# Moving the operands of the matrix products by 32 to 96 bytes in SBUF

## What is computed

```
for l in range(DEPTH):                       # DEPTH = 2
    h = hybrid_mixer(x, w_in[l], ...)        # three branches, three gates, one output projection
    x = layer_norm(alpha * x + h, ...)
    h = memory_cross_attention(x, mem, ...)  # 4 heads of 256
    x = layer_norm(alpha * x + h, ...)
    h = conv_ffn(x, ffn_w_in[l], ...)        # 1024 -> 2 x 2816 -> 1024, 3-tap convolution on the gate
    x = layer_norm(alpha * x + h, ...)
return _layer(x, mem_2, positions_2, ...)    # another mixer with three branches, then a wider conv FFN
```

## Time and profile before

| | |
|---|---|
| median of three executions | 1826.69 us |
| the profiled execution | 1827.95 us |
| its span, first to last instruction | 1826.3 us |
| its mean granted TensorE clock | 0.968 of full speed |
| TensorE matmul busy | 93% |
| VectorE busy | 65% |
| ScalarE busy | 51% |
| DMA engines | 46.3% in the weights' queue |
| HBM read | 296.38 MB |

### The profile page before, as it was taken

The page is one execution under the profiler, slowest core; times in us unless marked ns, Lnnn a source line. Parts: engine busy times, 40 slices in busy tenths (PEclk is TensorE's granted clock), DMA queues, the critical chain, the costliest instruction groups (busy, mean ns, idle before and its releaser), DMA issues.

```text
span 1826.3 us, 33070 instructions
## 1 busy us (share of the span) xinstructions
PE 1698.0 (93%) x12778; PEld 1604.2 (88%) x12778; DVE 1190.9 (65%) x1696; ACT 935.0 (51%) x1365; POOL 128.5 (7%) x83
## 2 busy tenths in 40 slices
PE   6999999998999799999999899987999889979998
PEld 6998899987999799888998799977899889979997
DVE  5676678557656776666864766677654554767676
ACT  4446645544444445664444454455575457355554
POOL 5310002002000210000110200011000000000000
PEclk9999999998999899999999899997999999989999
DMA  8843455534565354445553455534435443445652
GB/s 270 233 160 128 142 187 188 178 128 140 183 203 190 129 201 151 135 132 171 167 206 104 148 179 195 196 127 144 146 132 186 151 139 128 153 151 183 200 184 101
DMA packets 81668, 299.75 MB, mean 164 GB/s; under 512 B 10560, under 2 KB 10688, under 8 KB 80096
## 3 DMA queue, kind: packets, MB, share of 16 engines
q1 hardware_dynamic: 76720, 279.44, 46.3%
q0 software_dynamic: 4784, 18.11, 3.5%
HBM read 296.38 MB, written 4.19 MB: 165 GB/s over the span
## 4 chain that ended last, share of the span: by engine, by line
PE 79%; DVE 10%; ACT 5%; issue 5%; DMA 1%; DVEq 0%; ACTq 0%; SPq 0%
PE general L606 50%; PE general L610 13%; PE scores L641 5%; DVE weights_lo L1330 3%; PE scores L703 2%; PE attention_out L761 2%; ACT weights_hi L966 2%; PE attention_out L641 2%; PE probs_transposed L641 2%; DVE xT_hi_part L1349 1%; PE probs_transposed L722 1%; ACT exp_ring L1008 1%; PE general L658 1%; DVE softmax_stats L1457 1%; DMA attention_area<-in_mem 1%
## 5 line engine op out<-in xcount | busy, mean ns | idle before, releaser
L1330 DVE TENSOR_TENSOR weights_lo<-raw_weights,weights_hi 128x1024 fp32r<-128x1024 f32 x521 | 658.9, 1280 | 463.1 <-ACT weights_hi L966 459.5
L966 ACT ACTIVATE weights_hi<-raw_weights 128x1024 fp32r<-128x1024 f32 x521 | 548.7, 1057 | 436.0 <-PE general L606 266.2
L606 PE MATMUL general<-xT_hi_part,weights_hi 128*128 128x256 f32 x2432 | 692.0, 285 | 32.2 <-DVE xT_lo_part L1340 24.5
L606 PE MATMUL general<-xT_hi_part,weights_lo 128*128 128x256 f32 x2432 | 684.4, 281 | 0.0
L606 PE MATMUL general<-xT_lo_part,weights_hi 128*128 128x256 f32 x2432 | 684.0, 281 | 0.0
L606 PEld LDWEIGHTS general<-xT_hi_part,weights_hi 128*128 128x128 f32 x2432 | 462.5, 190 | 47.5 <-issue 40.9
L606 PEld LDWEIGHTS general<-xT_lo_part,weights_hi 128*128 128x128 f32 x2432 | 463.0, 190 | 1.4
L606 PEld LDWEIGHTS general<-xT_hi_part,weights_lo 128*128 128x128 f32 x2432 | 463.2, 190 | 0.0
L1606 DVE SCALAR_TENSOR_TENSOR exp_ring<-general,param_cols,exp_ring 128x255 f32<-128x255 f32 (+1 forms) x176 | 76.8, 478 | 55.4 <-ACT exp_ring L1127 53.8
L977 ACT ACTIVATE attention_area<-general 128x512 f32<-128x512 f32 x74 | 44.0, 596 | 93.7 <-PE general L606 64.7
L1846 POOL TENSOR_TENSOR x_tok<-z_tok,attention_area 128x1024 f32<-128x1024 f32 x14 | 36.8, 2630 | 732.4 <-DVE z_tok L1375 732.4
(11 more groups left out here) (250 smaller groups left out, 3009.9 us busy)
## 6 DMA issues: line engine op xcount, KB each, us to landing
raw_weights<-in_stream SPq DMA_DIRECT2D x525, 512.0 KB, 3.9
attention_area<-in_ln_rows POOLq DMA_DIRECT2D x9, 1024.0 KB, 5.0
bias_scratch<-in_rpb POOLq DMA_DIRECT2D x32, 96.0 KB, 9.2
attention_area<-bias_scratch POOLq DMA_DIRECT2D x2, 1536.0 KB, 8.8
z_tok<-in_x SPq DMA_DIRECT2D x1, 1024.0 KB, 5.1
attention_area<-in_mem SPq DMA_DIRECT2D x1, 1024.0 KB, 9.9
attention_area<-in_mem POOLq DMA_DIRECT2D x1, 1024.0 KB, 8.9
out_x<-x_tok SPq DMA_DIRECT2D x2, 512.0 KB, 2.6
```

Of the source, the lines that this page charges most:

```text
L606: ins = nc.tensor.matmul(ps[b][0:m, half * T:half * T + T], w[wk][:, half * m:half * m + m], x[xk_], start=first, stop=last, skip_group_ch ...
L966: nc.scalar.activation(hi_half(h), raw_half(h), ACT.Copy).then_inc(*hi_done.more())
L1330: nc.vector.tensor_tensor(lo_half(h), raw_half(h), hi_half(h).bitcast(F32), ALU.subtract).then_inc(*lo_done.more())
```

## The change

It takes away the two holes `stagger` (16 elements, 64 bytes) and `area_stagger` and puts five others in their place. Nothing else differs: every instruction, wait and transfer is the same, with other SBUF addresses.

```
-        sizes = (("raw", RAW * HALF_N), ("w_hi", SPLIT * HALF_N), ("w_lo", SPLIT * HALF_N), ("stagger", 16),
-                 ("x", 2 * D), ("z", 2 * D),
-                 ("xT_hi", 2 * D), ("xT_lo", 2 * D), ("memT", 2 * D), ("big", 24 * T), ("y", 12 * T),
-                 ("exp", 3 * 1152), ("pT", 4 * 512), ("const", CONST_N), ("col", COL_N), ("area_stagger", 16),
+        sizes = (("raw", RAW * HALF_N), ("w_hi", SPLIT * HALF_N), ("w_lo", SPLIT * HALF_N), ("x", 2 * D), ("z", 2 * D),
+                 ("gap_0", 8), ("xT_hi", 2 * D), ("gap_1", 16), ("xT_lo", 2 * D), ("memT", 2 * D), ("gap_2", 8),
+                 ("big", 24 * T), ("gap_3", 8), ("y", 12 * T),
+                 ("exp", 3 * 1152), ("pT", 4 * 512), ("const", CONST_N), ("col", COL_N), ("gap_4", 16),
                  ("area", 48 * T),
                  ("stat", 24), ("nst", 112))
```

## The result

The changed kernel is slower: 1840.0 us, the median of 5 executions (1837.53 to 1842.27), against 1824.34 us of the kernel before (1817.08 to 1826.84, 5 executions). The ratio is 1.009, with a 95% interval of 1.0075 to 1.0106. I had forecast 1819 us. The span of the profiled execution went from 1826.3 to 1835.9 us.

What follows compares the result with a forecast made beforehand. TensorE's matmuls bound the kernel, busy 1698.0 of 1826.3 us. The area gave -7.9 us and all else zero: 1827.95 - 7.9 = 1820.1 for the profiled execution, 1819 us for the median, range 1793 to 1842.

Steps and rivals of the forecast that it cites:

- What bounds the kernel: Whole kernel: TensorE busy 1698.0 of 1826.3 us; the change acts only through how long operations take at other addresses.
- (a): `attention_area` from 448 to 32: down, `merged`, `memory_out` go quick, first and third branch slow; sum -7.9 us.
- the sign of the distance: Split products: moving operand 64 below the stationary mostly quick, 64 above mostly slow; 4.43 ns between the paces.
- Step (b): xT high and low parts to 32 and 96 above the weights: sign stays, so zero; ends -28 and +6 us.
- Step (c): `second_branch` to 160 above, the memory's parts to 128: zero, within -3 to +3 us.
- (d): Plain float32 matmuls show one pace, 216 ns for 256 columns: zero, 1 us either way.
- (e): VectorE: operations take 692 ns at either placement of operands, weight split keeps its addresses: zero.
- The third one: Every call now quick: off the 64-byte grid it loses the quick pace, 12.6 us more, 1839 us; chance 0.28.
- The first rival: All split products: distances do nothing, only how a stretch begins decides; 1826.7 us again; chance 0.27.
- The second (xT quick): xT products: unlike high and low distances make slow ones quick, 17 to 28 us less, 1791 to 1802; chance 0.16.

Runs made afterwards that it cites:

- The first map: Run of split products alone on TensorE, no other engine: 20 activation distances from the weights, 48 products each, six starts; 113.3 to 120.0 ns a product.
- both maps: Split products alone on TensorE: 20 activation distances, then 8 x 8 pairs of high and low distances; feature-major, only pair (192, 192) of 64 reached 113.3 ns.

## Why the prediction was wrong

**What bounds the kernel** held: only the pace of matmuls moved, and the count of it, 17.0 us, is of the size of the loss.

**The step that failed is (a), the area.** I had taken the sign of the distance from the way that the calls sorted in the trace, and priced down at 220 ns. It went from 229.4 to 233.0. `merged` and `memory_out` went up too. Instead of 7.9 us less, the area alone cost 9 us. No run came near the 220: the lowest that any map shows is 226.7. My sorting mixed tiles, and one tile's calls are not independent samples: a whole stretch inherits its pace. 448 and 64 are two distances, and I drew a rule over all the others from them. The first map shows 16 distances, and the sign gives no rule: 64 below (448) is quick, 32 and 96 below (480 and 416) are not, and 192 above does what 64 below does, as the pace repeats after 256 bytes.

**Step (b), xT, was put at zero** with ends of -28 and +6 us. It measured 6 us slower, at the upper end: every quick stretch went. "The sign stays the same" was no reason. The nearest row was at 64, and that row had two paces; at 32 and 96 only the slower of them exists.

**Step (c)** was put at zero within 3 us, and its run shows no difference; by the count it costs about 3. **Steps (d) and (e)** held: VectorE's groups of the earlier trace rows within 2 ns, the plain float32 matmuls without a second pace.

**The rivals.** The third one gave 1839 us and its place, every call that had been quick. The time and the place are what happened. Its price of 12.6 us for the lost quick calls agrees with the count, 12.6 of 17.0. Its reason, the 64-byte grid, is not what happened: all tiles on the grid at 128 cost 21 us. The quick pace appeared only at odd multiples of 64 with the weights' parts at 0, or 128 for the low ones. It also left out that 118.3 to 120.0 exist, and down's 233, which make about 4.5 us, a quarter of the loss. The first rival (distances do nothing) falls with both maps. The second (xT quick) falls for 32 and 96; at 192 it happens in part, as one FFN of the two layers was quick and the other slow. The first map, with no other engine running, shows 113.3 to 120.0 ns by distance alone, so whatever holds a product up is not another engine; whether it is between TensorE's own two reads, as I had read it, or elsewhere, no run here shows. The Trainium skill ("SBUF — State Buffer", SBUF: two separate sides) says that TensorE waits on no other engine at its port. The map doesn't contradict that; that placement therefore cannot matter was my inference, the page doesn't say it, and the maps refute it. The Trainium skill ("TensorE: Matmul & The Clock Gate", Back-to-back issue gap) gives N / 2.4 + 2.5 ns for an isolated matmul, by which 256 columns take an estimated 109.2. The maps reach it at no distance; their lowest is 113.3.

**The chances** were the larger fault than the sum: with a rule drawn from two distances, the case that every quick call is lost deserved more than 0.28. Before the change 64 and 448 were both odd multiples of 64; after it no tile is.

## What to carry to other kernels

For split products of 256 columns as here, the start of the moving operand against that of the stationary one (modulo 256 bytes) is worth up to 6% of a product's time, 113.3 to 120.0 ns. Measure it by itself with the kernel's own order of operands before cutting the arena, with many starts, and don't interpolate between the distances that happen to be in a trace. Where one group of identical instructions shows two paces in two layers, look at how each stretch begins before arguing from averages. And compare the granted clock of all executions, not of the profiled one alone, before you look for a missing gain elsewhere.

## What was unexpected of the hardware

- The pace repeats after 256 bytes, to 0.1 ns over the 8 distances of the first map, though a stationary operand is 512 bytes a partition.
- Two paces at one distance are held through long stretches. With all tiles at 192, one layer's FFN ran at 117.8 ns throughout (22 calls of 48 feature-major products, 1056), and the next at 113.3.
- The spread of executions may follow. Where quick paces are closed to the feature-major products, executions differ little: 1842.06 to 1844.83 us with all tiles at 128, 1837.53 to 1842.27 in the changed kernel. Where two are open they differ by 14 us, as 1818.15 to 1832.37 for the kernel before on one chip. That the paces vary between executions as they do between layers is my reading; only one execution of each kernel was profiled. It has a rival: the small spreads are of four and five executions, the large one of seventeen, and in those seventeen the granted clock goes with the time, 0.968 in the slowest (1832.37 us) and 0.972 to 0.974 in the five quickest.
- Plain float32 matmuls show none of this: 216 ns for 256 columns, before and after the change.
